# Five matmul products per weight tile in place of six, from the gate stage on: pieces of 280 and 240 tokens, one product of 480 columns, and a VectorE addition to join the sums

## The chip, the core and the metric

The kernel runs on one core of a Trainium2 chip. A core has TensorE (PE, matrix products into PSUM), VectorE (DVE), ScalarE (ACT), GpSimd (POOL) and SyncE (SP, here the queue that loads the weights). PSUM has eight banks of 512 fp32 values in each of 128 partitions. The metric is the device time of one execution in microseconds (us); lower is better. Comparisons count as a difference from 2%.

## The reference

One step of a one-layer hybrid decoder trunk, in fp32, for 512 prompt tokens and 8 sample tokens with their own convolution states (520 tokens in all; 1024 features, FFN width 2816).

```
h = RMSNorm(x) * g_mix
a_val, a_gate, b_B, b_C, b_x, g_A, g_B = split(h @ w_in)      # 7 x 1024 columns
v  = LayerNorm(causal_conv31(a_val * sigmoid(a_gate)) + bias)
yA = silu(v) @ w_a_out
yB = (b_B * causal_conv3(b_C * b_x)) @ w_b_out
x  = x + (sigmoid(g_A) * yA + sigmoid(g_B) * yB) @ w_o
h2 = RMSNorm(x) * g_ffn;  f_gate, f_up = split(h2 @ w_up)     # 2 x 2816 columns
x  = x + (silu(causal_conv3(f_gate)) * f_up) @ w_down
y  = RMSNorm(x) * g_final
```

It returns y and the new convolution states.

## The kernel before

Features lie on the partitions, the N = 520 tokens along the free dimension. Every matrix product is made of weight tiles of 128x128. fp32 accuracy is reached by splitting: each weight tile is kept as a high part `w_hi` (the value as float32r) and a low part `w_lo` (what is left), and each activation tile as two neighbouring tiles of `act` or `mid`, index 2k (high) and 2k + 1 (low). Three of the four products of parts are summed: high x high, high x low, low x high. The 520 tokens are cut in two halves of H = 260, each in its own PSUM bank, so a weight tile costs six products of 260 columns: four in `hi_pass` (L996), two in `lo_pass` (L1003). All are float32r and have their own weight load.

A **unit** (`unit`, L1009) makes one output tile of 128 features: for the KT = 8 input tiles the high passes of tiles 0 to 6, the low passes of tiles 0 to 6, then tile 7's. `midway` puts two statistics products of plain fp32 into some units, called by the line `mean_over_features` (L1050, the products are L1053). Units are numbered g through the whole kernel: G_MIX 0 to 31, G_B 32 to 39, G_BOUT 40 to 47, G_GATE 48 to 63 (the gates g_A and g_B, in turn), G_AOUT 64 to 71, G_O 72 to 79, G_UP 80 to 123 (f_gate and f_up, in turn). From G_DOWN on, each of 8 output tiles has four units with 6, 6, 5 and 5 of 22 input tiles, and transposes of the output tile before (`turn`, L1144) between them.

PSUM holds two units' sums: `acc(s)` (L218) is banks 0 and 1 or banks 2 and 3. A unit starts after the unit two before it has been evicted (semaphore `evicted`), and after its weights are split (`hi_done`; `lo_done` ahead of its last tile). It ends with `mm_done`.

Weights arrive in a ring of four slots. SyncE loads 512 KB a unit (`load`, L246) once `w_lo` of four units earlier is made; ScalarE makes `w_hi` for the unit four ahead (`hi_split`, L327) when a unit is done, VectorE then `w_lo` (`lo_split`, L624). Each engine runs its list strictly in order.

- Gate stage, ScalarE (`gate_step`, L473, and the loop after it): sigmoid of the sums into `gate_a` or `t1` (`evict`, L336), then `hi_split`. Beside it the LayerNorm of branch A runs: in steps 2 to 5 VectorE centres two tiles of v (L842) while ScalarE squares them (L487) and VectorE sums them (L827); at step 7 `root` (L829) makes 1/sqrt(variance + eps) with a VectorE reciprocal of 520 columns (L834); in steps 8 to 15 `swish` (L489) makes sigmoid (L493) and affine (L495) on ScalarE, and VectorE multiplies (L852), normalizes the next tile (L854) and makes the low part (L633).
- G_AOUT, G_O: VectorE evicts (L870, L884), adds or rescales, ScalarE makes the activation's high part, VectorE its low part, then the weights' split. `tiles_from` lets the next stage start tile by tile. At the start of G_UP `root` runs again for the second RMSNorm, before the first eviction.
- G_UP: VectorE evicts with a product by `rinv` (L906, L911), makes the width-3 convolution (`narrow`, L730 and L733) and the gated product.
- G_DOWN: `down_out` (L923) evicts with the residual (L927), `turn` transposes to token rows, and the last RMSNorm follows.

Of the kernel before, what the change touches and what calls it, by code (L numbers as in the profile page):

```python
# [33 lines left out]
def build(nc, x_prompt, x_sample, state_a, state_b, state_f, g_mix, w_in, conv_a_w, conv_a_b, ln_a_g, ln_a_b,  # L34
# [9 lines left out]
    H = N // 2  # L44
    PADA, PADB = WA - 1, WB - 1
# [27 lines left out]
    with ExitStack() as ctx:  # L73
# [15 lines left out]
        xT = sb("xT", [P, KT, N])  # L89

# [83 lines left out]
        hi_done, lo_done, mm_done, evicted = sem("hi_done"), sem("lo_done"), sem("mm_done"), sem("evicted")  # L174
        act_hi, act_lo, prod_done = sem("act_hi"), sem("act_lo"), sem("prod_done")
# [22 lines left out]

        def merged(i):

            return i + 3
# [16 lines left out]
        def acc(s):  # L218

            return psum[:, 2 * (s % 2):2 * (s % 2) + 2, 0:H]  # L220

# [101 lines left out]
        def _(sc):  # L323
# [265 lines left out]

            sc.wait_ge(y_sq_set, 1)  # L590
            for s in range(RING):
                down_split(0, s)
            with sc.Fori(0, KT // 2 - 1) as it:
                for par in range(2):
# [6 lines left out]
                    down_split(n + 1, 2)  # L601
                    down_split(n + 1, 3)
            for n in (KT - 2, KT - 1):
                sc.wait_ge(y_scaled, START + 2 * n + 2)
# [12 lines left out]
        def _(ve):  # L617
            for started in (y_scaled, u_done, conv_b, win_conv, vsum_done, ssum_done, yb_gated, prod_done, conv_f, act_lo):
                ve.sem_inc(started, START)
# [18 lines left out]


# [175 lines left out]
            def gate_step(it, s):  # L815
                g = G_GATE + RING * it + s
                if s % 2 == 1:
# [61 lines left out]
            with ve.Fori(0, KT // RING) as it:  # L879
                for s in range(RING):  # L880
                    i = RING * it + s
                    g = G_O + i
                    out_of_psum(g, g)
                    ve.tensor_tensor(halves(tile(xT, i)), acc(s), halves(tile(xT, i)), ALU.add).then_inc(evicted, 1)  # L884
# [12 lines left out]
            with ve.Fori(0, FT // 2) as it:  # L897
                for s in range(RING):
                    g = G_UP + RING * it + s
                    i = 2 * it + s // 2  # L900
                    out_of_psum(g, g)
                    if s % 2 == 0:
# [3 lines left out]
                        ve.tensor_tensor(halves(cx[:, PADB:PADB + N]), acc(s), halves(rinv), ALU.mult).then_inc(evicted, 1)  # L906
# [3 lines left out]
                    else:  # L910
                        ve.tensor_tensor(halves(up_n), acc(s), halves(rinv), ALU.mult).then_inc(evicted, 1)  # L911
# [56 lines left out]
        def _(pe):  # L968
# [34 lines left out]
            def lo_pass(s, rhs, a, j, k, stop):  # L1003
# [3 lines left out]
                return last  # L1007

# [95 lines left out]
            for step in range(KT):  # L1104
                unit(G_GATE + step, step % RING, act, midway={min(SQUARE_STEPS): mean, ROOT_STEP: variance}.get(step))
# [6 lines left out]
            with pe.Fori(KT // RING, 2 * KT // RING) as it:  # L1112
                for s in range(RING):
                    unit(G_GATE + RING * it + s, s, act)


            for first, rhs, a in ((G_AOUT, mid, S_V), (G_O, act, S_M)):
                with pe.Fori(0, KT // RING) as it:
                    for s in range(RING):
                        unit(first + RING * it + s, s, rhs, done=tiles_from(a))  # L1120
# [83 lines left out]
```

## Time and profile before

| what | us |
|---|---|
| median of 3 runs | 892.8 |
| lowest run | 892.14 |
| highest run | 1424.63 |
| the profiled execution, first to last instruction | 890.5 |

The median is 2.3 us above the profiled span. The profile's page gives shares for each engine, 40 slices of the span, the chain of work that ended last, and groups of instructions by line. The trace behind it answers for any stretch: which instruction ran when, what ended the idle time before it, and which chain of waits set the end. PE is the matmuls, PEld the weight loads that overlap them. A matmul's own duration holds pipeline time that overlaps with the next, so the price of a product is read from starts, not from durations.

### The profile page before, as it was taken

The numbers are of one execution on the slowest core, as the hardware profiler recorded it, in microseconds if no ns is written. First come the engines' busy times: TensorE is split into PE (matmuls) and PEld (weight loads), VectorE is DVE, ScalarE is ACT, GpSimd is POOL, SyncE is SP. The second block draws the span as 40 slices with busy tenths as digits, with TensorE's granted clock in tenths as the row PEclk, the third lists the DMA queues.
The fourth block names the chain that finished last, engine by engine and source line by source line (L and its number), as shares of the span: only waits on it lengthen the run. The fifth ranks groups of instructions, "written<-read, shape, count | busy, mean of one in ns | idle before, by whom it ended". The sixth has DMA issues, their size and how long they took to land.

```text
span 890.5 us, 19207 instructions
## 1 busy us (share of the span) xinstructions
PE 865.3 (97%) x7163; PEld 862.0 (97%) x7163; DVE 599.1 (67%) x891; ACT 344.7 (39%) x571; POOL 118.0 (13%) x84
## 2 busy tenths in 40 slices
PE   5999999999999999999999999999999999999994
PEld 4899999999999999999999999999999999999994
DVE  4889999999999955765555766666666665333222
ACT  5564646454342234663233423333333234222221
POOL 0274756566000000000000000000000000000000
PEclk8999999999999999999999999999999999999997
DMA  6523333333432333233333242233322323332302
GB/s 200 142 79 90 99 91 94 124 113 88 118 110 72 95 105 96 72 94 95 94 96 94 71 119 84 84 92 94 93 84 85 92 65 94 103 93 82 97 15 96
DMA packets 156266, 84.68 MB, mean 95 GB/s; under 512 B 2925, under 2 KB 154953, under 8 KB 156184
## 3 DMA queue, kind: packets, MB, share of 16 engines
q1 hardware_dynamic: 153176, 81.59, 31.0%
q10 hardware_dynamic: 3051, 2.56, 0.9%
q8 instruction: 26, 0.43, 0.2%
q14 instruction: 13, 0.11, 0.0%
HBM read 81.70 MB, written 3.51 MB: 96 GB/s over the span
## 4 chain that ended last, share of the span: by engine, by line
PE 92%; DVE 3%; DMA 1%; issue 1%; ACT 1%; SPq 0%; POOL 0%; DVEq 0%; ACTq 0%; POOLq 0%
PE psum L1000 60%; PE psum L1006 31%; DMA v<-in_x_prompt 1%; DVE psum L697 0%; PE psum L1148 0%; POOL act L312 0%; DVE tmp L671 0%; PE psum L1053 0%; SPq L243 0%; DMA tmp<-in_state_conv_a 0%; DVE y L964 0%; PE psum L1074 0%; DVE cx L671 0%; DVE y_b L730 0%; PE psum L1110 0%
## 5 line engine op out<-in xcount | busy, mean ns | idle before, releaser
L1000 PE MATMUL psum<-act,w_hi 128*128 128x260 f32 x2752 | 364.0, 283 | 4.8 <-DVE act L675 3.3
L1000 PEld LDWEIGHTS psum<-act,w_hi 128*128 128x128 f32 x2752 | 343.3, 189 | 6.3 <-issue 3.6
L629 DVE TENSOR_TENSOR w_lo<-raw,w_hi 128x1024 fp32r<-128x1024 f32 (+2 forms) x156 | 188.5, 1210 | 93.7 <-ACT w_hi L334 93.3
L1000 PE MATMUL psum<-mid,w_hi 128*128 128x260 f32 x1920 | 249.5, 282 | 0.0
L1000 PEld LDWEIGHTS psum<-mid,w_hi 128*128 128x128 f32 x1920 | 238.1, 188 | 0.1
L334 ACT ACTIVATE w_hi<-raw 128x1024 fp32r<-128x1024 f32 (+2 forms) x156 | 157.0, 1007 | 193.2 <-PE psum L1006 193.1
L1006 PE MATMUL psum<-act,w_lo 128*128 128x260 f32 x1376 | 195.7, 282 | 0.0
L1006 PEld LDWEIGHTS psum<-act,w_lo 128*128 128x128 f32 x1376 | 177.9, 188 | 0.0
L1006 PE MATMUL psum<-mid,w_lo 128*128 128x260 f32 x960 | 135.1, 283 | 0.0
L1006 PEld LDWEIGHTS psum<-mid,w_lo 128*128 128x128 f32 x960 | 123.4, 188 | 0.0
L319 POOL TENSOR_TENSOR gate_a<-gate_a,prods 128x512 f32<-128x512 f32 x72 | 110.1, 1529 | 74.1 <-ACT prods L389 65.7
L697 DVE SCALAR_TENSOR_TENSOR psum<-u,cst,psum 128x512 f32<-128x512 f32 x96 | 66.8, 746 | 0.0
L906 DVE TENSOR_TENSOR cx<-psum,u 128x520 f32<-128x520 f32 x22 | 15.4, 700 | 53.8 <-PE psum L1006 53.2
L389 ACT ACTIVATE prods<-u,cst 128x512 f32 x72 | 46.5, 712 | 0.0
L340 ACT ACTIVATE tmp<-psum 128x520 f32<-128x520 f32 x32 | 19.3, 602 | 63.4 <-PE psum L1006 63.4
L719 DVE SCALAR_TENSOR_TENSOR v<-u,cst,v (+1 forms) x96 | 40.1, 479 | 0.7 <-DVE cx L795 0.5
L345 ACT ACTIVATE act<-tmp 128x520 f32 x30 | 19.2, 640 | 49.3 <-DVE tmp L873 34.5
L733 DVE SCALAR_TENSOR_TENSOR tmp<-cx,u,tmp 128x512 f32<-128x512 f32 (+1 forms) x66 | 36.1, 575 | 0.4
L556 ACT ACTIVATE tmp<-tmp 128x520 f32<-128x520 f32 x22 | 14.1, 643 | 51.1 <-DVE tmp L733 51.1
L911 DVE TENSOR_TENSOR u<-psum,u 128x520 f32<-128x520 f32 x22 | 15.4, 700 | 21.5 <-PE psum L1006 21.5
L633 DVE TENSOR_TENSOR act<-tmp,act 128x520 f32 x30 | 20.9, 697 | 8.4 <-ACT act L345 8.4
L927 DVE TENSOR_TENSOR tmp<-psum,xT 128x520 f32<-128x520 f32 x8 | 5.6, 700 | 25.5 <-PE psum L1006 25.5
(139 smaller groups left out, 414.6 us busy)
## 6 DMA issues: line engine op xcount, KB each, us to landing
raw<-in_w_in SPq DMA_DIRECT2D x56, 512.0 KB, 3.8
raw<-in_w_up SPq DMA_DIRECT2D x44, 512.0 KB, 3.8
raw<-in_w_down SPq DMA_DIRECT2D x16, 384.0 KB, 3.1
raw<-in_w_down SPq DMA_DIRECT2D x16, 320.0 KB, 3.0
raw<-in_w_b_out SPq DMA_DIRECT2D x8, 512.0 KB, 3.9
raw<-in_w_a_out SPq DMA_DIRECT2D x8, 512.0 KB, 3.5
raw<-in_w_o SPq DMA_DIRECT2D x8, 512.0 KB, 3.5
v<-in_x_prompt SPq DMA_DIRECT2D x4, 512.0 KB, 5.1
```

The lines of the kernel that those rows point to most:

```text
L319: pool.tensor_tensor(part, part, prods[:, k - 1, :], ALU.add).then_inc(pool_sum, 1)
L334: sc.activation(w_hi[:, s, 0:k, :], raw[:, s, 0:k, :], ACT.Copy).then_inc(hi_done, 1)
L340: sc.activation(halves(out), acc(s), func).then_inc(evicted, 1)
L345: sc.activation(out, src, ACT.Copy).then_inc(act_hi, 1)
L389: sc.activation(out, tile(u, i, k, k + SEQ), ACT.Copy, scale=scal(cst, i, C_WA + k)).then_inc(prod_in, 1)
L629: ve.tensor_tensor(w_lo[:, s, 0:k, :], raw[:, s, 0:k, :], w_hi[:, s, 0:k, :], ALU.subtract).then_inc(lo_done, 1)
L633: ve.tensor_tensor(out, src, hi, ALU.subtract).then_inc(act_lo, 1)
L697: ve.scalar_tensor_tensor(out=tile(v, i, 0, SEQ) if k == MIX_N - 2 else out, in0=src, scalar=w, in1=out, op0=ALU.mult, op1=ALU.add).then_i ...
L719: ve.scalar_tensor_tensor(out=out, in0=src, scalar=w, in1=out, op0=ALU.mult, op1=ALU.add).then_inc(dve_tap[group], 1)
L733: ve.scalar_tensor_tensor(out=out, in0=src, scalar=wk, in1=out, op0=ALU.mult, op1=ALU.add).then_inc(done, 1)
L1000: pe.matmul(a[:, h, :], w_hi[:, s, j, :], rhs[:, 2 * k + part, h * H:(h + 1) * H], start=start and part == 0, stop=False)
L1006: last = pe.matmul(a[:, h, :], w_lo[:, s, j, :], rhs[:, 2 * k, h * H:(h + 1) * H], start=False, stop=stop)
```

## The change

From the gate stage on, `wide_unit` takes the place of `unit`. The 520 tokens are cut in NA = 280 and NB = 240. `wide(s)` is a row of 760 columns over the two banks of a slot: columns 0 to 279 are the last 280 of the first bank (tokens 0 to 279), 280 to 519 the first 240 of the second bank (tokens 280 to 519), 520 to 759 the next 240 of the second bank, a separate sum. One product with `w_hi` takes the 240 tokens of the activation's high tile and those of its low tile as 480 columns (two stretches 520 columns apart) and writes both sums. So a weight tile has five products: 280 (high), 480 (high and low), 280 (low), and with `w_lo` 280 and 240.

The separate sum has to be added. ScalarE copies it from PSUM to the SBUF tile `low` (`copy_low`), VectorE adds `low` to columns 280 to 519 in PSUM (`join`), and the eviction, as before on ScalarE in the gate stage and on VectorE behind it, waits for `joined`. `low` is one buffer, so a copy waits for the join before. Evictions read the 520 columns as one stretch in place of two halves. The order of the other work in each engine's list is kept; in the gate stage VectorE's `join` stands at the start of `gate_step`, behind the LayerNorm's work of that step.

```diff
+    NA = 280
+    NB = N - NA
+        low = sb("low", [P, NB])
+        low_copied, joined = sem("low_copied"), sem("joined")
+        def join_of(g):
+            return START + g - G_GATE + 1
+        banks = psum[:, :, :].rearrange("p b n -> p (b n)")
+        def wide(s, lo=0, hi=None):
+            at = 2 * (s % 2) * 512 + 512 - NA
+            return banks[:, at + lo:at + (N if hi is None else hi)]
...
+            def copy_low(g, t, s):
+                sc.wait_ge(mm_done, g + 1)
+                sc.wait_ge(joined, join_of(t - 1))
+                sc.activation(low[:, :], wide(s, N, N + NB), ACT.Copy).then_inc(low_copied, 1)
+            def evict_wide(g, s, out, func):
+                copy_low(g, g, s)
+                sc.wait_ge(joined, join_of(g))
+                sc.wait_ge(evicted, out_of(g - 1))
+                sc.activation(out, wide(s), func).then_inc(evicted, 1)
...
                 if s % 2 == 0:
-                    evict(g, s, tile(gate_a, i), ACT.Sigmoid)
+                    evict_wide(g, s, tile(gate_a, i), ACT.Sigmoid)
                 else:
                     sc.wait_ge(yb_gated, START + i)
-                    evict(g, s, t1, ACT.Sigmoid)
+                    evict_wide(g, s, t1, ACT.Sigmoid)
                 hi_split(g + RING, s)
...
+                    copy_low(G_AOUT + i, G_AOUT + i, s)
                     act_hi_split(tile(act, 2 * i), t2, prod_done, START + KT + i + 1)
...
+                    copy_low(G_O + i, G_O + i, s)
                     sc.wait_ge(ssum_done, START + KT + i)
...
+                    copy_low(g, g, s)
                     hi_split(g + RING, s)
                     if s % 2 == 0:
...
+            def down_low(n, par):
+                copy_low(G_DOWN + RING * n + RING - 1, G_DOWN + n, par)
...
+            def join(g, t, s):
+                ve.wait_ge(mm_done, g + 1)
+                ve.wait_ge(low_copied, t - G_GATE + 1)
+                ve.tensor_tensor(wide(s, NA, N), wide(s, NA, N), low[:, :], ALU.add).then_inc(joined, 1)
+            def out_of_join(g, t, s):
+                join(g, t, s)
+                ve.wait_ge(evicted, out_of(t - 1))
+                ve.wait_ge(joined, join_of(t))
...
             def gate_step(it, s):
                 g = G_GATE + RING * it + s
+                join(g, g, s)
                 if s % 2 == 1:
...
-                    out_of_psum(g, g)
+                    out_of_join(g, g, s)
                     ve.wait_ge(prod_done, START + KT + i)
-                    ve.tensor_tensor(halves(t1), acc(s), halves(tile(gate_a, i)), ALU.mult).then_inc(evicted, 1)
+                    ve.tensor_tensor(t1, wide(s), tile(gate_a, i), ALU.mult).then_inc(evicted, 1)
...
             def down_out(n, par):
-                ve.wait_ge(mm_done, G_DOWN + RING * n + RING)
-                ve.wait_ge(evicted, out_of(G_DOWN + n - 1))
+                out_of_join(G_DOWN + RING * n + RING - 1, G_DOWN + n, par)
                 ve.wait_ge(y_turned, START + n)
-                ve.tensor_tensor(halves((t0, t1)[par]), acc(par), halves(tile(xT, n)), ALU.add).then_inc(evicted, 1)
+                ve.tensor_tensor((t0, t1)[par], wide(par), tile(xT, n), ALU.add).then_inc(evicted, 1)
...
+            def hi_wide(s, rhs, d, j, k, start):
+                pe.matmul(wide(d, 0, NA), w_hi[:, s, j, :], rhs[:, 2 * k, 0:NA], start=start, stop=False)
+                pe.matmul(wide(d, NA, N + NB), w_hi[:, s, j, :], rhs[:, 2 * k:2 * k + 2, NA:N], start=start, stop=False)
+                pe.matmul(wide(d, 0, NA), w_hi[:, s, j, :], rhs[:, 2 * k + 1, 0:NA], start=False, stop=False)
+            def lo_wide(s, rhs, d, j, k, stop):
+                pe.matmul(wide(d, 0, NA), w_lo[:, s, j, :], rhs[:, 2 * k, 0:NA], start=False, stop=stop)
+                return pe.matmul(wide(d, NA, N), w_lo[:, s, j, :], rhs[:, 2 * k, NA:N], start=False, stop=stop)
```

`wide_unit` has the order and the waits of `unit`, with `hi_wide` and `lo_wide` for `hi_pass` and `lo_pass`. The evictions of G_O and G_UP change as that of G_AOUT does. `down_low` stands ahead of ScalarE's fourth weight split of each column of G_DOWN.

## Rows read from the trace of the kernel before

**Rows 1.** The page: busy time, granted clock by slice, chain by engine.

```profile
PE 865.3 (97%) x7163; PEld 862.0 (97%) x7163; DVE 599.1 (67%) x891; ACT 344.7 (39%) x571; POOL 118.0 (13%) x84
...
PEclk8999999999999999999999999999999999999997
...
PE 92%; DVE 3%; DMA 1%; issue 1%; ACT 1%; SPq 0%; POOL 0%; DVEq 0%; ACTq 0%; POOLq 0%
```

**Rows 2.** Stages: length, busy us (instructions) by engine, granted clock, DMA share, GB/s.

```profile
305.55:406.61 101.06, 101.06 (x849) 100.65 (x848) 62.32 (x82) 51.06 (x71) 0.00 (x0) 1.00 0.32 94
498.30:747.00 248.70, 248.70 (x2074) 248.59 (x2074) 163.51 (x263) 78.90 (x111) 0.00 (x0) 1.00 0.30 87
```

**Rows 3.** Chain that ended last, one FFN unit: start us, us, what, products.

```profile
580.12 3.35 PE psum L1000 x28
583.46 1.69 PE psum L1006 x14
585.15 0.48 PE psum L1000 x4
585.63 0.24 PE psum L1006 x2
585.87 3.35 PE psum L1000 x28
```

**Rows 4.** The same chain: 19-column transposes, and fp32 products of 260 columns.

```profile
329.38 1.49 PE psum L1110 x22
...
353.31 0.88 PE psum L1053 x4
```

**Rows 5.** Weight loads in order of time, and a line's durations (min/median/max ns).

```profile
330.80 0.30 PEld L1000 LDWEIGHTS psum<-act,w_hi 128*128 128x128 f32 x2
...
L1006 PEld LDWEIGHTS psum<-act,w_lo x1376: 187/188/193, 33.5 to 877.1; 128*128 128x128 f32 x197
```

**Rows 6.** Durations of two lines, ns: ScalarE out of PSUM, VectorE with two SBUF inputs.

```profile
L432 ACT ACTIVATE tmp<-psum x8: 371/372/372, 219.8 to 260.4; 128x240 f32<-128x240 f32 x8
...
L777 DVE TENSOR_TENSOR tmp<-tmp,cst x8: 409/410/411, 223.0 to 263.8; 128x248 f32<-128x248 f32 x8
```

**Rows 7.** VectorE in order of time, a unit of G_AOUT; in brackets the idle time before.

```profile
412.62 0.70 DVE L870 TENSOR_TENSOR tmp<-psum,gate_a 128x520 f32<-128x520 f32 x1 [1.09 <-PE psum L1006]
413.53 0.70 DVE L873 TENSOR_TENSOR tmp<-tmp,y_b 128x520 f32<-128x520 f32 x1 [0.21 <-DVE tmp L870]
...
416.00 1.23 DVE L629 TENSOR_TENSOR w_lo<-raw,w_hi 128x1024 fp32r<-128x1024 f32 x1
```

**Rows 8.** ScalarE in order of time: two evictions of steps 4 and 5, two later ones.

```profile
337.82 0.59 ACT L340 ACTIVATE gate_a<-psum 128x520 f32<-128x520 f32 x1
...
343.88 0.59 ACT L340 ACTIVATE tmp<-psum 128x520 f32<-128x520 f32 x1
...
369.55 0.81 ACT L495 ACTIVATE v<-v,cst 128x520 f32<-128x520 f32 x1
370.26 0.58 ACT L340 ACTIVATE tmp<-psum 128x520 f32<-128x520 f32 x1
...
375.76 0.58 ACT L340 ACTIVATE gate_a<-psum 128x520 f32<-128x520 f32 x1
```

**Rows 9.** Step 7: the chain at the unit's end, and VectorE's last work of the root.

```profile
354.92 3.35 PE psum L1000 x28
...
359.70 0.64 DVE L847 TENSOR_TENSOR v<-v,u 128x520 f32<-128x520 f32 x1
```

**Rows 10.** Start of G_UP: VectorE's first eviction, and the chain at unit 82.

```profile
504.29 0.70 DVE L906 TENSOR_TENSOR cx<-psum,u 128x520 f32<-128x520 f32 x1 [0.58 <-DVE cx L892]
...
505.22 3.45 PE psum L1000 x28
```

**Rows 11.** VectorE's last eviction, in order of time.

```profile
877.52 0.70 DVE L927 TENSOR_TENSOR tmp<-psum,xT 128x520 f32<-128x520 f32 x1 [10.61 <-PE psum L1006]
```

More of the change, by code:

```diff
@@ L617, in _ @@
         def _(ve):
-            for started in (y_scaled, u_done, conv_b, win_conv, vsum_done, ssum_done, yb_gated, prod_done, conv_f, act_lo):
+            for started in (y_scaled, u_done, conv_b, win_conv, vsum_done, ssum_done, yb_gated, prod_done, conv_f, act_lo, joined):
                 ve.sem_inc(started, START)
@@ L882, in _ @@
                     g = G_O + i
-                    out_of_psum(g, g)
-                    ve.tensor_tensor(halves(tile(xT, i)), acc(s), halves(tile(xT, i)), ALU.add).then_inc(evicted, 1)
+                    out_of_join(g, g, s)
+                    ve.tensor_tensor(tile(xT, i), wide(s), tile(xT, i), ALU.add).then_inc(evicted, 1)
                     ve.wait_ge(act_hi, S_H + i + 1)
@@ L900, in _ @@
                     i = 2 * it + s // 2
[L901 removed]
+                    out_of_join(g, g, s)
                     if s % 2 == 0:
@@ L910, in _ @@
                     else:
-                        ve.tensor_tensor(halves(up_n), acc(s), halves(rinv), ALU.mult).then_inc(evicted, 1)
+                        ve.tensor_tensor(up_n, wide(s), rinv, ALU.mult).then_inc(evicted, 1)
                         ve.wait_ge(evicted, out_of(g))
@@ L1007, in lo_pass, with wide_unit @@
                 return last
+            def hi_wide(s, rhs, d, j, k, start):
[5 more added lines that the diff above has]
+                return pe.matmul(wide(d, NA, N), w_lo[:, s, j, :], rhs[:, 2 * k, NA:N], start=False, stop=stop)
+            def wide_unit(g, s, rhs, t=None, dst=None, ks=range(KT), first=True, final=True, done=None,
+                          midway=None):
+                t = g if t is None else t
+                d = s if dst is None else dst
+                if first:
+                    pe.wait_ge(evicted, out_of(t - 2))
+                pe.wait_ge(hi_done, g + 1)
+                end = len(ks) - 1
+                for j, k in enumerate(ks):
+                    if j == end:
+                        pe.wait_ge(lo_done, g + 1)
+                        for jj in range(end):
+                            lo_wide(s, rhs, d, jj, ks[jj], False)
+                        if midway is not None:
+                            midway()
+                    if done is not None:
+                        pe.wait_ge(*done(k))
+                    hi_wide(s, rhs, d, j, k, first and j == 0)
+                lo_wide(s, rhs, d, end, ks[end], final).then_inc(mm_done, 1)
             def unit(g, s, rhs, t=None, dst=None, ks=range(KT), first=True, final=True, done=None,
@@ L1104, in _ @@
             for step in range(KT):
-                unit(G_GATE + step, step % RING, act, midway={min(SQUARE_STEPS): mean, ROOT_STEP: variance}.get(step))
+                wide_unit(G_GATE + step, step % RING, act, midway={min(SQUARE_STEPS): mean, ROOT_STEP: variance}.get(step))
                 if step == min(SQUARE_STEPS) + 1:
@@ L1113, in _ @@
                 for s in range(RING):
-                    unit(G_GATE + RING * it + s, s, act)
+                    wide_unit(G_GATE + RING * it + s, s, act)
             for first, rhs, a in ((G_AOUT, mid, S_V), (G_O, act, S_M)):
@@ L1119, in _ @@
                     for s in range(RING):
-                        unit(first + RING * it + s, s, rhs, done=tiles_from(a))
+                        wide_unit(first + RING * it + s, s, rhs, done=tiles_from(a))
             def mean_square():
@@ L1127, in _ @@
             for s in range(RING):
-                unit(G_UP + s, s, mid, done=tiles_from(S_H), midway=mean_square if s == 0 else None)
+                wide_unit(G_UP + s, s, mid, done=tiles_from(S_H), midway=mean_square if s == 0 else None)
             with pe.Fori(1, FT // 2) as it:
                 for s in range(RING):
-                    unit(G_UP + RING * it + s, s, mid)
+                    wide_unit(G_UP + RING * it + s, s, mid)
             pe.wait_ge(fg_tail, START + FT)
@@ L1153, in down @@
                 for s in range(RING):
-                    unit(G_DOWN + RING * n + s, s, act, t=G_DOWN + n, dst=par,
+                    wide_unit(G_DOWN + RING * n + s, s, act, t=G_DOWN + n, dst=par,
                          ks=range(KFIRST[s], KFIRST[s] + KSPLIT[s]), first=s == 0, final=s == RING - 1,
```

7 lines of the change are left out of this document (6 added, 1 removed).

## Prediction

> **What bounds the kernel now.** I read the page first [rows 1]: TensorE is busy 97% of the span, the chain that ended last runs 92% of its length through TensorE, almost all of it in the two lines of the products, and the granted clock is full in 37 slices of 40. Then the stages [rows 2]: in both stretches TensorE is busy all the time at granted clock 1.00, its 2.4 GHz level, while VectorE is busy 62% and 66%, ScalarE 51% and 32%, and the DMA share is 0.30 to 0.32. So the price of a product sets the time as long as the helpers keep up, and the second question is whether they still do. For the price I took the chain of waits in the FFN stage [rows 3]: a unit is 28 + 14 + 4 + 2 = 48 products, and one unit starts 5.75 us after the other (580.12 to 585.87): 119.8 ns a product. Its 28 first ones take 3.35 us, 119.6 ns each; with this figure the six of a weight tile cost 717.5 ns, a unit 5.74 us.
>
> **Why 119.6 ns, and what another width would cost.** 260 columns at 2.4 GHz are 108.3 ns. What the other 11 ns are decides this case, and the trace holds no product of the new widths. The nearest rows [rows 4]: four plain fp32 products of 260 columns take 0.88 us, 220 ns each, which is 520 column times (216.7 ns) and only 3.3 ns more, although each of them loads weights too. 22 tiny transposes with 19 columns take 1.49 us, 68 ns each, far above their 8 ns of columns: there it is the loading of weights that paces. And where TensorE starts a unit just after those [rows 5], two weight loads together take 0.30 us, of which one load's record is 0.188: the second began 0.11 us after the first, with no full stream running. So a weight load alone costs about 110 ns, about what 260 columns cost, and more than that is plausible while columns are being read. I take it that today's product is paced by the load of the next weights at 119.6 ns, and that a product long enough to hide the load costs its columns and the 3.7 ns or so of the fp32 row.
>
> The five products are then: 280 columns (116.7 + 3.7 = 120.4, about the load's 119.6), three times; 240 columns, paced by the load, once; together 4 x 119.6 = 478.4. The 480 columns are 200 + 3.7 = 203.7. Sum 682.1 ns for 717.5: 35.4 ns less per weight tile. Bounds: if the 240 columns cost only a load alone (110) and the long product nothing beyond its columns (200), with 119.6 for the other three, it is 669, the low end. The high end is no saving (rival 2). Of the two ends the middle value is nearer to the rows of loads and fp32 products.
>
> **What the change touches.** 16 + 8 + 8 + 44 units of 8 tiles and 8 times 22 tiles, 784 tiles. It adds to each of 84 output tiles a ScalarE copy of 240 columns from PSUM and a VectorE addition of 240 columns. Near forms stand in the trace [rows 6]: 0.372 us (240 columns out of PSUM) and 0.410 us for a VectorE operation of 248 columns in SBUF, 0.40 for 240; that it works in PSUM should cost nothing, as 520 columns take 0.70 us from PSUM and from SBUF [rows 7]. The evictions keep their 520 columns and their price. The copy stands ahead of the addition, the addition ahead of the eviction: 0.37 + 0.04 + 0.40 + a wait on the own semaphore of 0.21 (the gap of [rows 7]) is 1.02 us more from the end of a unit to its evicted tile where VectorE evicts, and 0.37 + 0.04 + 0.40 + 0.05 = 0.86 us where ScalarE does. No DMA is added or moved; SyncE's loads wait for the splits of four units earlier and stay some units ahead.
>
> **Gate stage, where this is on a chain.** In steps 8 to 15 the two helpers form a ring: VectorE's product of v, ScalarE's high part, sigmoid, affine, eviction, split of the weights, VectorE's split, the next product. Its period is read from two evictions [rows 8]: 370.26 to 375.76, 5.50 us, just under TensorE's 5.74. The copy goes in between the affine (ends 370.36) and the eviction, and VectorE's addition behind it, so the period becomes 5.50 + 0.86 = 6.36 us, over TensorE's new 8 x 0.682 = 5.46. TensorE may run only two units ahead (two pairs of banks), so it falls to 6.36 us a unit. In steps 2 to 5 the ring of centring and squares has a period of 6.06 us (337.82 to 343.88) and gets 6.9; the slack of a unit and the 1.4 us of transposes in there absorb most of it, 0.9 us of waiting is left at unit 7. At step 7 VectorE stands in the reciprocal until 360.34 [rows 9], 5.4 us after that unit's end (354.92); the eviction did not need VectorE and now does: 5.41 + 0.40 + 0.05 + 0.59 = 6.5 us against 5.46, 1.1 us of waiting. Sum over the 16 gate units and the first behind them: nine units at 5.46 (49.1), 1.8 of statistics products and 1.4 of transposes inside them, 0.9 waited, then 1.1 + 5.46, then seven at 6.36 (44.5), and 0.3 for the even and odd steps' semaphores: 104.6, say 104.9 with the start's latency. It was 101.06, from 305.55 to 406.61 [rows 2]. This stretch becomes 3.9 us slower.
>
> **Behind it.** Output of branch A: VectorE's work of a unit, from the eviction's start (412.62) to the end of the split (416.00 + 1.23) is 4.61 us [rows 7], with the addition 5.22, under 5.46: hidden, but with 0.2 us to spare. The same holds for the w_o stage. FFN: VectorE goes from 66% to (163.5 + 44 x 0.40) / 236, 77%, hidden. At the turn to the FFN the root chain holds VectorE until 504.29 [rows 10]; then the addition comes first, so the first eviction ends 0.61 later, and TensorE arrives 0.33 earlier: 0.95 us more of waiting (some 0.1 is there now, 3.45 for 3.35). Down: 22 tiles to a column, helpers half idle, hidden. At the end nothing covers it [rows 11]: VectorE waits 10.61 us for the last products and evicts at 877.52; 1.03 us more.
>
> Sum: 784 - 17 x 8 = 648 tiles x 35.4 = 22.9 gained; 3.9 + 0.95 + 1.03 = 5.9 lost; 17.0 us net. The profiled span of 890.5 becomes 873.5. The median of the runs, 892.8, is 2.3 above that span (start and end around it): 892.8 - 17.0 = 875.8.
>
> **Rivals.** (1) The 11.3 ns are a fixed price of each product. Then a tile costs 650 + 5 x 11.3 = 706.2: 648 x 11.3 ns = 7.3 gained, the gate stretch loses 4.6, the rest 1.8: 892. For it: the surplus of the fp32 row is not nought either. Against: it is 3.3 and not 11.
>
> (2) The columns set the price, 0.46 ns each, and the number of products doesn't matter: 280 + 480 + 280 + 280 + 240 = 1560 = 6 x 260. Nothing is gained, the ring of the gate stage costs 5.2, the turn to the FFN 0.6 and the end 1.03: 899.6, slower than before. It decides as soon as the saving per tile is below 10 ns. For it: a product is never seen below 119.6 at full clock. Against: the fp32 products read the same 260 columns of four bytes with 3.3 ns surplus, and the two loads of [rows 5]. The Trainium skill (TensorE: Matmul & The Clock Gate, Back-to-back issue gap) gives columns / 2.4 + 2.5 ns for a product at full clock, 110.8 ns for 260 columns, and by it the tile would go from 665 to 662.5 ns, nearly this rival's result; the trace's 119.6 does not agree with its level.
>
> (3) A new form is slow: the 480 columns come from two stretches 2,080 bytes apart, and 240 is short. At the two column times of the fp32 row, 480 columns cost 404 ns, 200 more per tile, 157 us in all: about 1030. No row speaks for it but the want of one.
>
> **How the numbers follow.** Load-paced, as forecast: 0.60; (1) 0.18; (2) 0.13; (3) 0.09. Forecast 875.8. Within the first case the tile's low end, 669, gives 648 x 48.5 = 31.4 less 5.5, 866.9, and chains that cost 4 us more than I count give 880, so its own range is 866 to 884. The range for all reaches to (2): 866 to 900, which leaves (3) and little else. A change under about 2% (17.9 us) is what a measurement of this kernel can hardly tell from none; the forecast, 1.9%, lies at that bound. Faster by over 2% needs below 874.9: a little under half of the first case, 0.29. Slower by over 2%: (3), 0.09. Within: 0.62.
>
> **What would show it.** In the chain of waits an FFN unit should start 5.46 us after the one before (rival 1: 5.65, rival 2: 5.74), its 480-column products some 204 ns apart. Gate evictions in steps 8 to 15 should stand 6.36 us apart, with TensorE idle 0.9 us before each unit; the lines of copy and addition should read 0.37 and 0.40. A wait before each unit of the w_o or FFN stage would show the helpers' rings mis-sized, and the forecast too low; it is wrong altogether if the short products fall below the load's time or the long one costs much over 204 ns.

## Result and the profile after

The changed kernel takes 899.88 us (median of 4, 899.67 to 900.19) against 893.05 of the kernel before on the same chip: 1.0076 times as long, interval 1.0061 to 1.0091. It is a little slower; 875.8 was forecast, with 866 to 900 as range. The time is that of the second rival (899.6), which had been given 0.13. The profiled span is 897.8 us, 7.3 more than before's 890.5. One run of the kernel before, at 1424.63 us, stands apart as slow; all its others, here and beside the experiments, lie between 892.14 and 894.07.

From the page of the kernel after, the busy times and the chain by engine, which answer to [rows 1]:

```profile
PE 867.1 (97%) x6379; PEld 838.2 (93%) x6379; DVE 633.4 (71%) x975; ACT 370.5 (41%) x655; POOL 117.5 (13%) x84
...
PE 86%; DVE 5%; issue 3%; ACT 3%; DMA 1%; SPq 0%; POOL 0%; DVEq 0%; ACTq 0%; POOLq 0%
```

784 products are gone, and TensorE's busy time has not fallen: 867.1 for 865.3. There are fewer products, and each is dearer. Part of the chain has moved from TensorE (92 to 86%) to its helpers.

Two stretches in the kernel after, to set beside [rows 2]. The first has the length of the gate stage (its units end 0.28 us later on the chain, at 306.52 and 413.57); the second begins and ends within units, as that of [rows 2] does (length; busy time and count of PE, PEld, DVE, ACT, POOL; granted clock; DMA share; GB/s):

```profile
306.24:413.30 107.06, 103.16 (x712) 96.80 (x711) 67.72 (x97) 56.40 (x87) 0.00 (x0) 1.00 0.29 86
498.90:747.00 248.10, 247.79 (x1725) 236.92 (x1725) 180.92 (x303) 92.58 (x155) 0.00 (x0) 1.00 0.30 88
```

The gate stage takes 107.06 us where it took 101.06, and TensorE idles 3.9 of them. In the FFN the clock is full, TensorE idles 0.31 of 248.10 us, and nothing is gained. Where the 7.3 us of span come from: 1.0 lies ahead of the gate stage, in unchanged code (the stage begins at 306.52 for 305.55 on the chain), 6.0 in the gate stage, -0.6 from there to the last product, and 0.9 behind it. No run says where the 1.0 comes from: from TensorE's first instruction to its first product of the gate stage the profiled executions of the eight whole kernels, which have the same code there, take 302.56 (before) to 304.39 us, this one 303.51. So times from that product to TensorE's last instruction are the cleaner measure: 573.44 us before, 579.79 after, 6.35 more.

The chain through one FFN unit after [rows 3] (start us, us, what; the lines are 280 columns L1063, L1065, L1069, then 480 columns L1064; pieces between them left out):

```profile
574.21 0.13 PE psum L1069
...
575.78 0.22 PE psum L1064
...
579.95 0.13 PE psum L1069
```

From one L1069 to the one a unit later: 5.74 us, as before. Every 480-column product holds the chain for 0.22 us (203.7 ns were forecast), every product of 280 for 0.13 (119.6 in the forecast's sum). Start to start over the FFN stage they take 219 and 128 to 131 ns and the one of 240 takes 110.8: 3 x 129 + 219 + 111 = 717 ns, and six products took 717.5.

### The profile page after: what moved, and what is told of

Its sections match the earlier page's. It is cut to its first block, busy times and chain, and to the rows that moved or that the text cites. A ratio compares the mean times of both kernels' runs of the same rounds, so it can differ in the third digit from the quotient of the medians.

```text
span 897.8 us, 18032 instructions
## 1 busy us (share of the span) xinstructions
PE 867.1 (97%) x6379; PEld 838.2 (93%) x6379; DVE 633.4 (71%) x975; ACT 370.5 (41%) x655; POOL 117.5 (13%) x84
## 4 chain that ended last, share of the span: by engine, by line
PE 86%; DVE 5%; issue 3%; ACT 3%; DMA 1%; SPq 0%; POOL 0%; DVEq 0%; ACTq 0%; POOLq 0%
PE psum L1052 18%; PE psum L1064 17%; PE psum L1063 10%; PE psum L1069 10%; PE psum L1065 10%; PE psum L1058 9%; PE psum L1070 9%; DMA v<-in_x_prompt 1%; ACT w_hi L349 1%; DVE u L887 1%; ACT v L523 1%; DVE tmp L905 1%; DVE v L907 0%; DVE psum L749 0%; DVE psum L684 0%
## 5 line engine op out<-in xcount | busy, mean ns | idle before, releaser
L1052 PE MATMUL psum<-act,w_hi 128*128 128x260 f32 x1280 | 169.3, 285 | 4.3 <-DVE act L727 3.3
L1052 PEld LDWEIGHTS psum<-act,w_hi 128*128 128x128 f32 x1280 | 160.9, 191 | 5.2 <-issue 3.6
L1064 PE MATMUL psum<-mid,w_hi 128*128 128x480 f32 x416 | 158.8, 382 | 0.0
L1064 PE MATMUL psum<-act,w_hi 128*128 128x480 f32 x368 | 139.9, 380 | 0.0
L1063 PE MATMUL psum<-mid,w_hi 128*128 128x280 f32 x416 | 121.7, 292 | 0.7 <-ACT gate_a L368 0.4
L1065 PE MATMUL psum<-mid,w_hi 128*128 128x280 f32 x416 | 120.8, 290 | 0.0
L1063 PE MATMUL psum<-act,w_hi 128*128 128x280 f32 x368 | 109.6, 298 | 3.5 <-ACT tmp L368 1.9
L1065 PE MATMUL psum<-act,w_hi 128*128 128x280 f32 x368 | 106.7, 290 | 0.0
L1069 PE MATMUL psum<-mid,w_lo 128*128 128x280 f32 x416 | 105.7, 293 | 0.0
L1070 PE MATMUL psum<-mid,w_lo 128*128 128x240 f32 x416 | 103.6, 273 | 0.0
L1069 PE MATMUL psum<-act,w_lo 128*128 128x280 f32 x368 | 94.1, 292 | 0.0
L1058 PE MATMUL psum<-act,w_lo 128*128 128x260 f32 x640 | 89.6, 284 | 0.0
L1063 PEld LDWEIGHTS psum<-mid,w_hi 128*128 128x128 f32 x416 | 78.1, 188 | 10.4 <-ACT gate_a L368 0.6
L1069 PEld LDWEIGHTS psum<-mid,w_lo 128*128 128x128 f32 x416 | 78.2, 188 | 3.6
L1063 PEld LDWEIGHTS psum<-act,w_hi 128*128 128x128 f32 x368 | 69.1, 188 | 13.1 <-ACT tmp L368 3.0
```

Of the source, the lines that this page charges most:

```text
L1052: pe.matmul(a[:, h, :], w_hi[:, s, j, :], rhs[:, 2 * k + part, h * H:(h + 1) * H], start=start and part == 0, stop=False)
L1058: last = pe.matmul(a[:, h, :], w_lo[:, s, j, :], rhs[:, 2 * k, h * H:(h + 1) * H], start=False, stop=stop)
L1063: pe.matmul(wide(d, 0, NA), w_hi[:, s, j, :], rhs[:, 2 * k, 0:NA], start=start, stop=False)
L1064: pe.matmul(wide(d, NA, N + NB), w_hi[:, s, j, :], rhs[:, 2 * k:2 * k + 2, NA:N], start=start, stop=False)
L1065: pe.matmul(wide(d, 0, NA), w_hi[:, s, j, :], rhs[:, 2 * k + 1, 0:NA], start=False, stop=False)
L1069: pe.matmul(wide(d, 0, NA), w_lo[:, s, j, :], rhs[:, 2 * k, 0:NA], start=False, stop=stop)
```

## What the runs were to tell apart

Two questions: whether the lost gain is in the price of a product or in the helpers, and, if it is the price, what makes it. The candidates are the columns themselves, a fixed price, the load of weights, or a fee for the second stretch of the 480-column product.

### The products alone

TensorE does nothing but blocks of 96 like products, each block one line:

```
for i in range(96):
    pe.matmul(psum[:, i % 2, 0:260], W(i), xr[:, 520 * (i % 7):520 * (i % 7) + 260], ...)
```

> This kernel leaves the whole step out: it copies some inputs to the outputs and runs only TensorE, seventeen blocks of 96 products of one form each, with no other engine at work, so each form's price is read from the starts. Theory A (a float32r product is paced by reading its columns, 0.46 ns each, whatever the weights): 260 columns 119.6 ns, 512 columns 235.5, the two stretches of 240 221, 256 columns 117.8; 64 and 32 weight columns with 260 columns still 119.6; bf16 products of 260 columns, which read half the bytes, 111 or below. Theory B (loading the weights slows the columns that stream beside it): 64 weight columns 114, 32 weight columns 111, and bf16, whose weights load faster, near 111 as well; 512 columns 224, as the load takes only part of their time. Theory C (power: the array is slowed with real data): all-zero operands 111, everything else 119.6, bf16 too. Theory D (PSUM takes a sum every 0.46 ns): bf16 of 260 columns 119.6 and of 512 235. Short products (128, 64 columns) show the load alone: 108 to 112.

Its chain, whole blocks (L70 float32r 260 columns, L72 512, L74 480 in two stretches; L84 bfloat16 512; L88 260 columns with 64 columns of weights; L96 all zeros):

```profile
35.07 11.56 PE psum L70 x96
46.62 21.78 PE psum L72 x96
68.41 20.91 PE psum L74 x96
...
141.02 20.72 PE psum L84 x96
...
167.10 11.44 PE psum L88 x96
...
213.31 11.59 PE psum L96 x96
```

Divided by 96: 120.4 ns for 260 columns, 226.9 for 512, 217.8 for 480. The kernel's price of 119.6 is thus TensorE's own; nothing around it adds to it. It is no price of the load: with half or a quarter of the weight columns it stays 119, although the record of a load shrinks from 188 ns to 134 and 108; with the same weights each time it is 120.4. With half the rows it is 120.6 and with zeros 118.7, each without the block's first gap of 225 ns. Products of 128 columns take 111.1 ns (10.67 us for the block), and those of 64 take no less, some 112: there is a floor. That the floor is the load of the weights is the reading of [rows 5]; no block varied the load at a short product. bfloat16 products of 128 and 512 columns take 55.8 and 215.8 ns. A block of 96 plain fp32 products stands in the trace as 192 instructions, 219.2 ns each, so a product of the form of [rows 4] costs two of them.

Within the 64-column block the granted clock fell to half, the 1.2 GHz level, though TensorE had not paused: it had run 128-column products for 10.7 us and 64-column ones for 3.6. It stayed there into the next block, bfloat16 products of 260 columns. Two stretches, the start of the 64-column block and the time at the lower level (figures as above, without DVE):

```profile
111.51:115.10 3.59, 3.59 (x34) 3.59 (x34) 0.00 (x0) 0.00 (x0) 1.00 0.02 5
115.10:132.10 17.00, 17.00 (x82) 15.86 (x82) 0.00 (x0) 0.00 (x0) 0.50 0.00 0
```

The 112 ns for 64 columns come from the first stretch; at the lower level such a product took 213 ns. For bfloat16 with 260 columns the part at full clock, from 132.2 us on, gives 110.9 ns start to start.

The Trainium skill (TensorE: Matmul & The Clock Gate, Back-to-back issue gap) gives columns / 2.4 + 2.5 ns for an isolated product at full clock: 110.8 and 215.8 ns. The bfloat16 blocks agree to 0.1 ns, although they are streams with a load for each product; the float32r blocks lie 10 to 11 ns above it at both widths.

Two explanations were left for the float32r prices: the columns alone, or a fixed price with a fee for the second stretch. 480 columns in two stretches at 217.8 lie near the line from 260 to 512, but that line rests on two points, and a fee of some nanoseconds for the second stretch could hide in it.

### Widths and stretches

> As the first kernel of forms: the step is left out, blocks of 96 products of one form each, TensorE alone. The first one showed 120.4 ns for 260 columns, 226.7 for 512 (a surplus over columns at 2.4 GHz of 12 and 13.4 ns), 217.8 for 480 columns in two stretches (17.8), and no effect of half or a quarter of the weight columns. Theory E (a float32r product pays about 12 ns once, and about 5 to 9 more for every further stretch of its moving columns): 240 columns 112, 280 129, 380 170.5, 480 contiguous 212.5; 480 in two stretches 218 whether they lie apart or side by side is not clear (side by side in one row the access pattern may be merged: 212.5), in four 228, in eight 250, in sixteen 290. Theory A (0.46 ns a column): 110, 129, 175, 221 for 480 contiguous too, and stretches cost nothing. If the surplus belongs to reading four bytes a column, bf16 in two stretches stays at 202.5. Start address odd or aligned: no difference under E or A; a theory of lines read (64 bytes) would make the odd one slower by 3 to 7 ns.

The chain of its blocks (L70 240 columns, L72 280, L74 380, L76 480 in one stretch, L78 in two, L86 in sixteen; L88 and L90 bfloat16 480 in one and two):

```profile
34.61 10.79 PE psum L70 x96
45.40 12.39 PE psum L72 x96
57.79 16.72 PE psum L74 x96
74.50 21.03 PE psum L76 x96
95.53 20.91 PE psum L78 x96
...
179.77 22.40 PE psum L86 x96
202.17 19.45 PE psum L88 x96
221.63 19.44 PE psum L90 x96
```

112.4, 129.0, 174.2, 219.0 ns for 240 to 480 columns: from 280 to 480 each column more costs 0.45 ns, over a start of 3 to 6 ns, so each column costs 0.456 to 0.461 ns all told. A second stretch costs nothing (217.8 for 219.0), nor do four (217.6); eight cost 6 ns and sixteen 14. The fee has fallen. What is left for the change is arithmetic: 1560 columns in six products or in five, with one start less.

### Six products, with the copies and the additions of the change

```
-   pe.matmul(wide(d, 0, NA), w_hi..., rhs[:, 2 * k, 0:NA], ...)
-   pe.matmul(wide(d, NA, N + NB), w_hi..., rhs[:, 2 * k:2 * k + 2, NA:N], ...)
-   pe.matmul(wide(d, 0, NA), w_hi..., rhs[:, 2 * k + 1, 0:NA], ...)
+   hi_pass(...)          # the six products of before
-   sc.activation(low, wide(s, N, N + NB), ACT.Copy)
+   sc.activation(low, acc(s)[:, 1, 0:NB], ACT.Copy, scale=0.0)
```

> The six products of the kernel before, with the copies and additions of the change: ScalarE copies 240 columns times nought, VectorE adds them to the second half, in the same places and with the same waits. If the change's whole loss is the helpers' ring (products worth nothing either way), it takes what the changed kernel takes, 899 to 901 us, and the gate stage's units of steps 9 to 15 stand 6.4 us apart. If the five products cost something of their own it is faster than the changed kernel by that; if they save something hidden by the ring, slower, above 902.

901.93 us (901.42 to 902.16), ratio 1.0096 (1.0079 to 1.0113). So the helpers' work costs 8.8 us on the kernel before, and the five products give 2.1 back; the changed kernel differs from this one in them and in that its additions and evictions read one stretch in place of halves. From the first product of the gate stage on, in the profiles, it is 581.32 us: 7.9 for the helpers, 1.5 back for the products. Over 784 weight tiles that is 2 to 3 ns a tile, where 35.4 were forecast. The FFN unit is 5.75 us here, 3.35 of them its first 28 products:

```profile
571.38 3.35 PE psum L1052 x28
...
577.14 3.35 PE psum L1052 x28
```

### Five products, but not in the gate stage

```
-   wide_unit(G_GATE + step, step % RING, act, ...)
+   unit(G_GATE + step, step % RING, act, ...)
-   evict_wide(g, s, tile(gate_a, i), ACT.Sigmoid)      # copy, join, eviction
+   evict(g, s, tile(gate_a, i), ACT.Sigmoid)
```

> The changed kernel with the gate stage as it was: six products and no copy or addition in units 48 to 63, five products from unit 64 on. If the gate ring is the loss, 6.0 us come back: 899.9 - 6.0 = 893.9, within 1 us of the kernel before; what is left is the turn to the FFN (0.45) and the end (1.0) less the 13 ns by which a unit on mid is shorter with five products (0.7 in all). If the loss were in the products, only a fifth of it would come back: 898.5.

894.45 us (893.95 to 895.08), ratio 1.0015 (1.0005 to 1.0025): 5.4 us of the 6.8 come back with the gate stage. From its first product on it is 574.00 us, 5.8 less than the changed kernel and 0.6 more than the kernel before. Its chain runs through TensorE again without a gap, a unit 5.75 us after the other:

```profile
384.81 3.35 PE psum L1051 x28
...
390.56 2.51 PE psum L1051 x21
```

### The long product from one stretch

The same kernel, with the low part of each activation tile stored turned (tokens 280 to 519 first), so that they follow on those of the high part and the 480 columns are read in one stretch:

```
-   rhs[:, 2 * k:2 * k + 2, NA:N]
+   rhs[:, 2 * k:2 * k + 2, :].rearrange("p t n -> p (t n)")[:, NA:N + NB]
```

> The gate stage with six products as in the run before (894.45 us), and the low activation tile stored turned from the gate stage on: tokens 280 to 519 first, then 0 to 279, so that the 480 columns are one stretch (high tile 280 to 519, low tile's first 240). VectorE writes each low tile in two instructions for that. Theory E: 5 to 7 ns less per weight tile, 648 of them behind the gate stage and the first unit: 3.2 to 4.5 us, so 890 to 891.3, the first version under the 893.1 of the kernel before; the 480-column product stands 212 to 214 ns ahead of the next. Theory A: 894.5, nothing changes.

893.87 us (893.41 to 894.79), ratio 1.001 (1.0001 to 1.0019): 0.6 less than with two stretches and no faster than the kernel before. The fee's theory wanted 890 to 891.3; it has fallen inside the kernel too. Start to start the 480-column product takes 217.6 ns here and 219.7 with two stretches, where that theory had 212 to 214.

### Two bytes in place of four

If the columns set the price, and a bfloat16 column costs 0.417 ns where a float32r column costs 0.46, then the shape of the work can stay as it was, and the products with a low part should move to bfloat16. The kernel before, from the stage of w_o on (592 weight tiles):

```
+   sc.activation(w_16[:, s, 1, 0:k, :], w_hi[:, s, 0:k, :], ACT.Copy)          # w_hi in two bytes
+   sc.activation(half(t16, 2 * i + 1, 1), tile(t, 2 * i), ACT.Copy)            # high activations too
-   pe.matmul(a[:, h, :], w_hi[:, s, j, :], rhs[:, 2 * k + 1, h * H:(h + 1) * H], ...)
+   pe.matmul(a[:, h, :], w_16[:, s, 1, j, :], r16[:, 2 * k + 1, 0, h * H:(h + 1) * H], ...)
-   pe.matmul(a[:, h, :], w_lo[:, s, j, :], rhs[:, 2 * k, h * H:(h + 1) * H], ...)
+   pe.matmul(a[:, h, :], w_16[:, s, 0, j, :], r16[:, 2 * k + 1, 1, h * H:(h + 1) * H], ...)
```

> The kernel before (six products of 260 columns for each weight tile), but from the stage of w_o on (592 weight tiles) the four products with a low part read two-byte data: w_lo and the low parts of the activations are stored as bfloat16, with a bfloat16 copy of w_hi (ScalarE, one more copy per unit, 1.06 us by the copy that makes w_hi) and of each high activation tile (0.37 us) beside them, in the same room. The two products high x high stay float32r. Nothing is left out. The shape of the work is as before: six products, same widths, same order, no joins. Theory of the columns (a float32r column is read at 0.44 to 0.46 ns, a bfloat16 column at 0.417): four products of 110.8 ns in place of 119.6, so 8.8 x 4 x 592 = -20.8 us; 893.1 - 20.8 = 872.3, up to 1 more at the turns of the stages: 871.5 to 874. FFN units of eight tiles 8 x (2 x 119.6 + 4 x 110.8) = 5.46 us in place of 5.74. Rival, the weight load or a price by the product sets the pace, whatever the columns hold: no gain but for the copies' cost, 892 to 896, FFN units 5.74. Rival, a change of data type between neighbouring products costs something by itself: between the two, above 875, and the four units' time over 5.46 tells it.

883.74 us (883.48 to 883.88), ratio 0.9896 (0.988 to 0.9913): faster, but by less than half of what was expected. Its chain in the FFN (L1045 two float32r products, L1047 two bfloat16 ones, L1052 the bfloat16 pass of w_lo):

```profile
563.58 0.24 PE psum L1045 x2
563.82 0.24 PE psum L1047 x2
564.06 1.57 PE psum L1052 x14
```

14 bfloat16 products in a row take 1.57 us, 112 ns each, 8 below float32r. The bfloat16 pairs between float32r pairs take 0.24, as much as float32r. So 16 products of a unit got cheaper and 16 did not: 592 / 8 units x 16 x 8 ns = 9.5 us, the 9.35 measured. The expectation's third theory, a cost where the type changes, holds; the forecast of 872.3 was made without it.

### The same products, sorted

```
    for j in range(lo, hi): high_16(...)      # the float32r products of the unit
    for j in range(lo, hi): low_16(...)       # then its 32 bfloat16 products
```

> As the kernel with two-byte low products, but the order inside a unit is changed: first the 16 float32r products of its eight weight tiles, then the 32 bfloat16 ones (one unit at the turn to w_o's stage and one at the turn to the FFN keep their last tile apart). Nothing is left out, no product is added or removed. In the kernel with two-byte low products a group of two float32r and two bfloat16 products took 30.4 + 204.0 + 123.3 + 121.1 = 479 ns, as much as four float32r products, and products of the bfloat16 pass 111.6. Theory of the columns with a charge where the type changes: the bfloat16 products are cheap again once they stand together; an FFN unit 16 x 119.6 + 32 x 111.3 = 5.475 us, plus two changes of some 9 ns: 5.49 in place of 5.62; 592 weight tiles x (720 - ...)/8 by the unit: 74 units' worth x 0.13 = -9.6 us, so 883.7 - 9.6 = 874, 873 to 876. Rival, a bfloat16 product beside a new activation tile is as dear as a float32r one (the w_lo pass was cheap for another reason): no gain from the order, 883 to 885.

879.06 us (878.63 to 879.79), ratio 0.9843 (0.9827 to 0.9859). FFN units take 5.507 us, near the expected 5.49, but 3.9 us were lost at one place: the first FFN unit took 10.35 us for 6.50. Its chain (TensorE's parts and the wait), then its last two parts as stretches, with the granted clock as third figure from the end:

```profile
491.59 0.03 issue
491.62 0.08 DVEq L917
...
494.47 0.70 DVE u L860
495.18 0.14 issue
495.31 2.04 PE psum L1127 x4
497.35 3.88 PE psum L1051 x28
```

```profile
495.31:497.35 2.04, 2.04 (x5) 1.40 (x6) 1.23 (x1) 1.99 (x3) 0.00 (x0) 0.51 0.00 0
497.35:501.23 3.88, 3.88 (x30) 3.18 (x28) 3.14 (x2) 2.66 (x4) 0.00 (x0) 0.82 0.48 139
```

The mean of squares (L1127), which waits for VectorE's last running sum, stood ahead of the 28 bfloat16 products of seven tiles. Before, the low products of these tiles had hidden that wait. The wait is only half of the loss: from 491.60 to 495.30 TensorE idled 2.0 us, and then the granted clock fell, to 0.51 over the mean of squares and 0.82 over the 28 products. These took 2.04 and 3.88 us where the next kernel, at full clock, takes 0.90 and 3.15: 1.9 us more.

### Sorted, with the mean of squares behind the low products

> As the kernel with the sorted two-byte products, with one thing moved: in the first FFN unit the mean of squares (two sums over the features on TensorE, which wait for DVE's last running sum) comes behind the 28 bfloat16 products of the first seven tiles instead of ahead of them. Nothing is left out. In the sorted kernel TensorE stood from 491.59 to 495.31 us there and did these 28 products only at 497.35; the unit took 10.35 us where the one without sorting took 6.50. If that wait was all that the sorting lost, 3.2 us of products move under it and the unit goes to 6.5 to 7.2: 879.06 - 3.5 = 875.5, 875 to 876. If something else at the turn holds it (DVE's square sums, the eviction of the unit before), it stays at 878 to 879.

875.79 us (875.08 to 876.28), ratio 0.9805 (0.9789 to 0.9821), with 875.5 expected. The wait is gone and the clock stays full there, and an FFN unit is two pieces of 16 float32r and 32 bfloat16 products:

```profile
488.28 3.15 PE psum L1051 x28
...
496.96 0.90 PE psum L1127 x4
...
559.48 1.91 PE psum L1045 x16
561.40 3.59 PE psum L1051 x32
```

119.4 ns for a float32r product, 112.2 for a bfloat16 one, 5.51 us for the unit. This version is 17.3 us faster than the kernel before and 24.1 faster than the changed one, with ScalarE at 51% busy for 39. The interval of the ratio reaches to both sides of 2%. Its low parts carry fewer bits than those of the other two kernels, so it buys time with accuracy.

### Types mixed, and where a read starts

> The step is left out; blocks of 96 products on TensorE alone, each block one line. float32r and bfloat16 products of 260 columns mixed: alternating one by one, two by two, four by four, eight by eight, 16 and 32, 48 and 48; then float32r 512, 504, 480, 384 columns from starts at multiples of 512, 512 from starts 8 behind these, 320 from multiples of 520, and bfloat16 400. If a change of type has a charge c (each way, mean), the mean price of a mixed block of run length r is (120 + 111)/2 + c / r: with c = 9 ns 124.5 at one by one, 120.0 at two by two, 117.8 at four, 116.6 at eight, 115.7 at 48. If there is no charge, but a bfloat16 product costs what its neighbour costs, 120 in the short mixes and 115.5 in the long one. Widths: by the line 6 + 0.444 ns a column 384 costs 176.5, 320 148.1, 480 219, 504 229.8 and 512 233.3; if starts at multiples of 512 help (512 was 226.7 there), 504, 480 and 384 come out 6 ns below the line and 512 from the shifted starts on it. bfloat16 400: 0.417 x 400 + 2.5 = 169.3.

The chain of the mixed blocks (all of 260 columns: L70 float32r alone, L72 bfloat16 alone, L74 alternating one by one, L76 two by two, L78 four by four, L80 eight by eight, L82 16 and 32), then L86 512 columns from starts at multiples of 512, L88 from starts 8 further, L90 504 columns:

```profile
34.80 11.56 PE psum L70 x96
46.36 10.66 PE psum L72 x96
57.02 11.85 PE psum L74 x96
68.86 11.48 PE psum L76 x96
80.34 11.27 PE psum L78 x96
91.62 11.18 PE psum L80 x96
102.80 10.97 PE psum L82 x96
...
124.88 21.79 PE psum L86 x96
146.67 22.40 PE psum L88 x96
169.07 21.77 PE psum L90 x96
```

Divided by 96, a product costs 123.4 ns alternating one by one, 119.6 two by two, 117.4 four by four and 116.5 eight by eight, where the mean of the two prices is 115.7. By the number of changes of type in a block that is 7.7, 7.7, 6.7 and 5.8 ns for each, so a charge of some 6 to 8 ns a change describes them, as the expectation's first theory had it with 9. At 16 and 32 a product costs 114.3 for a mixture of 114.2, and so few changes would add about 0.3: that block can't tell. Two by two is what the unsorted kernel does, and its groups of four took 479 ns, 119.8 a product: two changes at 7.7 ns take back 15 of the 19 ns that its two bfloat16 products save. As for the starts: 512 columns from shifted starts cost 233.3 ns, on the line of 6 + 0.444 ns a column, from multiples of 512 226.9, as much as 504 columns there. 480 gain only 2.3 (216.7), and 384 lie 3.2 below that line (173.3). Why the steps lie where they lie, no run shows, nor why 512 columns with 64 columns of weights took 230.0 ns from the same starts in the run before.

## Why the prediction was wrong

**The price of a product: the step that failed.** The prediction took the 11.3 ns over 260 columns as the time of the next weights' load, and let a longer product keep only the 3.7 ns of the fp32 row. The blocks show no load in this price, and a line through 280, 380 and 480 columns in which the surplus grows with the width: 129.0 for the forecast 119.6, 219.0 for 203.7. Term by term, a weight tile is 3 x 129 + 219 + 111 = 717 where 682.1 were summed; of the 35.4 ns x 648 tiles = 22.9 us forecast as gained, 1.5 to 2.1 came (the kernel with six products and the joins against the changed one). The 240 columns are the one term that was cheaper than its 119.6: they took 110.8, near the 110 of the low bound.

**The two rows that misled.** The 110 ns that [rows 5] gave for a load fit the floor of the short products, 111 to 112 ns. But 119.6 lies above it; "more than that is plausible" turned the load into the bound without a row. The 68 ns of the transposes, read in the same breath as the pace of a load, did not fit that price either. [Rows 4] gave 3.3 ns of surplus for fp32 products, and from that it was inferred that four-byte columns cost nothing beyond the clock. That form runs at another rate and said nothing on float32r. The four records are also not four products but two: `mean_over_features` issues two, and each stands there as two instructions, as the 192 for 96 above show. So a plain fp32 product of 260 columns costs some 440 ns, about four column times, and not two. The row outweighed the plain reading that no product was ever seen under 119.6. (A slip on which nothing rests: [rows 1] have the full clock in 38 slices, not 37.)

**The ring of the gate stage: right in kind.** Forecast 6.36 us a unit; it is 6.40. ScalarE's copies in order of time in the kernel after, which answer to [rows 8]:

```profile
366.86 0.81 ACT L523 ACTIVATE v<-v,cst 128x520 f32<-128x520 f32 x1
367.57 0.35 ACT L361 ACTIVATE low<-psum 128x240 f32<-128x240 f32 x1
368.47 0.61 ACT L368 ACTIVATE gate_a<-psum 128x520 f32<-128x520 f32 x1 [0.55 <-DVE psum L684]
...
373.98 0.35 ACT L361 ACTIVATE low<-psum 128x240 f32<-128x240 f32 x1
```

From copy to copy 6.41; the sigmoid stands 0.55 us for the addition each time, as foreseen (0.40 of addition and its waits). The stage lost 6.0 us where 3.9 were forecast and rival 2 had 5.2: since the products had not become cheaper, nothing in the stage offsets what a slower unit costs over 5.74, and units 57 and 58 took 6.69 and 6.71 (end to end) instead of 6.4. Of the 0.9 us of waiting foreseen at unit 7 only 0.2 came (units 54 and 55, start to start: 12.57 us for 12.36). The kernel with six products and the joins has the same lengths (6.69, 6.69, then 6.38 to 6.42), so they are the helpers' and not the products'.

**The helpers' prices: right, their whole cost too low.** In the kernel after (line, busy, mean ns, idle before):

```profile
L684 DVE TENSOR_TENSOR psum<-psum,low 128x240 f32<-128x240 f32 x84 | 34.9, 416 | 100.0 <-ACT low L361 99.6
...
L361 ACT ACTIVATE low<-psum 128x240 f32<-128x240 f32 x84 | 30.9, 368 | 115.9 <-PE psum L1070 113.6
```

416 ns for the forecast 400, 368 for 372 [rows 6]. That the addition works in PSUM cost next to nothing. Elsewhere they are hidden, as forecast: in the FFN VectorE is busy 180.92 of 248.10 us, 73%, and no unit waits after the turn. All in all the helpers cost 7.9 us from the gate stage on (8.8 by the medians) where 5.9 were summed, most of the excess in the gate stage.

**The turn and the end.** At the turn to the FFN 0.45 us were lost (unit 82 takes 6.31 for 5.86), less than the forecast 0.95, near rival 2's 0.6. At the end the addition stands ahead of the last eviction; answer to [rows 11]:

```profile
884.33 0.42 DVE L684 TENSOR_TENSOR psum<-psum,low 128x240 f32<-128x240 f32 x1 [11.06 <-ACT low L361]
884.84 0.70 DVE L979 TENSOR_TENSOR tmp<-psum,xT 128x520 f32<-128x520 f32 x1
```

Copy, addition and wait cost 0.9 us there (1.03 forecast).

**The rivals.** Rival 2 came true in mechanism and place. That it also meets the time to 0.3 us is partly luck: the gate stage cost 0.8 us more than it had, 1.0 us of the profile's difference lies in unchanged code, and 1.5 to 2.1 came back from the products, where it had nothing. Rival 1 falls with the widths: a fixed price of 11.3 would have given 480 columns 211 ns. Rival 3 falls with the stretches: two are free. The chances were wrong, not the cases. Rival 2 had 0.13 on the strength of one row of another form.

## What to carry to other kernels

Where TensorE is busy all the time, merging products pays only what each product costs beyond its columns; measure two widths of the very form, in the very type, before counting a surplus as fixed. A split into high and low parts can give its low products a smaller type, which here saved 1.95% at the price of bits, if products of one type stand together and what had been hidden between them finds other cover. An addition to a helper that is 50% busy is not free where helpers form a ring: its latency, not its busy time, set the pace. And a short wait of TensorE can cost more than itself, when the granted clock falls behind it.

## What the runs showed of the hardware

- A float32r product costs 0.444 to 0.455 ns a column plus a start of some 3 to 6 ns at full clock: 112.4 ns at 240 columns, 129.0 at 280, 174.2 at 380, 219.0 at 480. bfloat16 costs columns / 2.4 + 2.5: 110.9 at 260, 169.3 at 400, 215.8 at 512.
- float32r products with 128 x 128 weights have a floor of 111 to 112 ns (64 and 128 columns); that it is the load's is likely and not shown. A bfloat16 product of 128 columns takes 55.8.
- A plain fp32 product of 260 columns runs as two instructions of 219 ns each.
- Moving columns may come from up to four stretches at no cost; eight cost 6 ns and sixteen 14 ns at 480 columns.
- Neighbouring products of different type (float32r and bfloat16, 260 columns) cost some 6 to 8 ns a change, in runs of one to eight.
- float32r reads from multiples of 512 columns are 6.4 ns cheaper than from shifted starts at 512 columns and 2.3 at 480.
- The granted clock fell to 0.50 for 17 us while TensorE ran without a pause, in a block of float32r products with 64 columns. It also fell, with four statistics records and 28 bfloat16 products taking 5.9 us for 4.05, behind a stretch of 3.7 us in which TensorE idled 2.0.

The reason for the dearer float32r column stays open: the price is measured, and at 260 columns zeros, half the rows, fewer or repeated weights and a single bank change it by less than 2 ns.
